# Up projections of a conv-GLU feed-forward layer by seven half-size products, in a float32 kernel on one NeuronCore

## The chip, the cores and the metric

One Trainium2 chip, one of its cores. The kernel computes two model blocks one behind the other in float32, in one launch. The metric is device microseconds of one execution of the program, from repeated runs; a smaller number is better. The chip's engines that occur here: TensorE (PE; its weight loads are listed as PEld), VectorE (DVE), ScalarE (ACT), GpSimd (POOL) and SyncE (SP), whose queue issues the DMAs.

## The reference

The first block (attention, retention and a mixture of experts) is not touched. The second block has two layers on 512 tokens of width 1024; each layer is a mixer, a layer norm, and the feed-forward part that the change is about:

```python
DEPTH_2 = 2; D_MODEL = 1024; SEQ = 512; D_FF = 2816; FFN_CONV = 3

def conv_glu_ffn(x, w_up, w_fconv, b_fconv, w_down):
    a, g = jnp.split(x @ w_up, 2, axis=-1)        # x [1, 512, 1024], w_up [1024, 5632]
    g = causal_dwconv(g, w_fconv, b_fconv)        # three taps along the tokens, per channel
    return (jax.nn.silu(g) * a) @ w_down          # w_down [2816, 1024]

h = layer_norm(ALPHA * h + mix, ln1_g[l], ln1_b[l])
f = conv_glu_ffn(h, w_up[l], w_fconv[l], b_fconv[l], w_down[l])
h = layer_norm(ALPHA * h + f, ln2_g[l], ln2_b[l])
```

`a` are called the values, `g` the gates, and `silu(g) * a` the hidden rows. Everything is float32.

## The kernel before, in words

Five engines run their own instruction lists, held together by semaphores. In `layers_block` each engine goes through the two layers in the same order: mixer, layer norm, feed-forward part (`pe_ffn`, `act_ffn`, `dve_ffn`, then `pool_down` and `dve_down`). `need(name, n)` waits until a semaphore has reached n in this layer, and does so once for each value. `own.do(ins)` waits on VectorE for an instruction of its own; `own(ins)` only counts it.

**Up projections.** The inner dimension of 2816 is cut into NJ = 22 tiles of 128 channels. `m.aT` holds the layer norm's result transposed, as 8 blocks (KT) of 128 input channels by 512 tokens. For tile j, `pe_ffn` (matmul at L2571) runs 8 matmuls for the gates into one bank and 8 for the values into another, each with 128x128 of w_up as the weights and 512 tokens as columns: 16 matmuls. A float32 matmul appears in the trace as two weight loads and two matmul records. Tiles use banks 0 and 1, or 2 and 3, in turn; TensorE waits for `f_gcopy` (gates copied) and `f_hid` (hidden row made) of two tiles before. In tile 0 the last 128 tokens come apart, behind the layer norm's last transposes. At the end of a tile's gates TensorE raises `f_g`, at the end of its values `f_a`.

ScalarE (`act_ffn`) copies the gates to `m.gp` (L2625), and makes SiLU of the convolution's result in `m.gs` (L2629). VectorE (`dve_ffn`) makes the convolution with three instructions (L2641 to L2643), and the hidden row `m.hidT[:, j, :]` with one (L2649), which reads the values from their bank. GpSimd is idle after it has finished the layer norm's rows (L1909, L1910, `pool_ln_rows`).

**Weights.** The SP queue (`sp_ffn`) loads w_up in 11 chunks of two tiles, 2 x 1024 KB each (L2474, L2475), into three slots in turn; chunk c waits for `f_a` of tile 2(c-3)+1. Rows (of 128 channels) 10 to 21 of w_down come as chunks 11 to 13 of 2048 KB through the same slots (L2480), chunk 13 after the last tile; rows 0 to 9 (KE = 10) come behind chunk 4, as 3584 and 1536 KB into `m.wd` (L2482, L2483).

**Down products.** They are already made by seven products of halves: the table SEVEN gives for each product which halves (of tokens, of the inner dimension) of the left operand are added or subtracted, which halves (inner dimension, output) of the right one, and to which quarters of the result the product goes with which sign. Products are accumulated over 11 pairs of rows, in the order `pairs(i)`; a pair is two matmuls of 512 columns, four records. VectorE sums halves of hidden rows (`dve_hid_sums`, L2686; the first four pairs already in tile 10), GpSimd sums halves of weights (`pool_down`, L2667, after the last hidden row, with six buffers `m.bsum` that lie over the convolution's buffers), VectorE adds the products from the banks to `m.h` (`dve_down`, L2704, L2706). Product i uses banks 4 and 5, 6 and 7, 2 and 3, 0 and 1 in turn. The matmul is at L2593.

## Time and profile before

| | us |
|---|---|
| runs: median of 3 (lowest, highest) | 3326.09 (3324.59, 3326.73) |
| profiled execution, its own time | 3328.42 |
| its span | 3326.6 |
| PE busy, share of span | 2857.9, 86% |
| DVE, ACT, POOL busy | 751.8, 462.2, 408.2 |
| mean granted TensorE clock | 0.928 |

The profile has a page (busy time of each engine, 40 slices of the span, DMA queues, the chain of work that ended last, the costliest groups of instructions) and a trace that can be asked by line, by stretch and in order of time. Times count from the span's start. Matmuls are pipelined and the ends of their records are modelled, so the spacing of their starts says more than their durations. A granted clock of 1.00 is 2.4 GHz, 0.50 is 1.2 GHz. The layers' up projections stand at about 2155 to 2461 and 2876 to 3182 us, the down products behind each.

### The profile page before, as it was taken

Reading aid. Unit: us, or ns where it says so; the run is one execution under the profiler, and the core shown is the slowest. Engines: PE = TensorE matmul, PEld = TensorE weight load, DVE = VectorE, ACT = ScalarE, POOL = GpSimd, SP = SyncE. Lnnn points to the kernel's source line nnn. Section 1 sums busy time; section 2 is a strip of 40 time slices with the busy share of each in tenths; the row PEclk is TensorE's granted clock in tenths of the full one; section 3 lists DMA queues with packets and bytes.
Section 4 is the critical chain, followed back from the end, with each engine's and each line's share of the span. In section 5 each row is a group of like instructions: output and inputs, shape, how many; then the busy total and the mean of one; then the engine's idle time right before and its main releaser. Section 6 shows DMA issues by size and latency. Waiting matters only on the chain. (4 is left out here: it accounts for less than half of the span.)

```text
span 3326.6 us, 29164 instructions
## 1 busy us (share of the span) xinstructions
PE 2857.9 (86%) x11870; PEld 1567.5 (47%) x11870; DVE 751.8 (23%) x1885; ACT 462.2 (14%) x1050; POOL 408.2 (12%) x357
## 2 busy tenths in 40 slices
PE   8999999999856565565655899999999999999998
PEld 7888666446722232222322654444444655444443
DVE  2222222101401010010010423322134224212145
ACT  1222232110100000000000223110000222100000
POOL 1101023100100000000000400110026200200044
PEclk9999999999877787777877998999999998999999
DMA  5111221121599999999999511132210311142200
GB/s 210 58 71 71 77 77 51 63 76 57 232 428 428 428 429 428 428 428 428 429 428 427 181 65 64 42 131 79 93 61 0 128 53 50 56 143 92 81 34 25
DMA packets 142087, 592.74 MB, mean 178 GB/s; under 512 B 17186, under 2 KB 88354, under 8 KB 114722
## 3 DMA queue, kind: packets, MB, share of 16 engines
q1 hardware_dynamic: 134674, 574.56, 43.6%
q10 hardware_dynamic: 5120, 8.39, 0.7%
q0 software_dynamic: 2192, 8.39, 0.7%
q8 instruction: 70, 1.15, 0.1%
q14 instruction: 31, 0.25, 0.0%
HBM read 572.37 MB, written 16.84 MB: 177 GB/s over the span
## 5 line engine op out<-in xcount | busy, mean ns | idle before, releaser
L2571 PE MATMUL bank<-arena 128*128 128x512 f32 (+2 forms) x1472 | 608.9, 576 | 9.1 <-DVE arena L1866 9.1
L1240 PE MATMUL bank<-arena 128*32 128x512 f32 x2048 | 294.6, 739 | 347.2 <-DMA arena<-in_moe_w 346.1
L2571 PEld LDWEIGHTS bank<-arena 128*128 128x128 f32 x1472 | 275.8, 191 | 340.3 <-issue 330.4
L429 PE MATMUL bank<-arena 128*128 128x384 f32 x1280 | 431.8, 490 | 1.0 <-PEq L861 1.0
L429 PEld LDWEIGHTS bank<-arena 128*128 128x128 f32 x1280 | 297.9, 238 | 105.9 <-issue 6.0
L1240 PEld LDWEIGHTS bank<-arena 128*32 128x32 f32 x2048 | 81.3, 132 | 559.8 <-issue 559.8
L2593 PE MATMUL bank<-arena 128*128 128x512 f32 x616 | 265.2, 592 | 0.0
L1985 PE MATMUL bank<-arena 128*128 128x512 f32 (+3 forms) x736 | 251.2, 499 | 1.5 <-DVE arena L1866 1.5
L2667 POOL TENSOR_TENSOR arena<-arena 128x512 f32<-128x512 f32 x110 | 148.5, 1355 | 636.0 <-DVE arena L2649 579.1
L1985 PEld LDWEIGHTS bank<-arena 128*128 128x128 f32 x736 | 138.2, 190 | 103.5 <-issue 70.0
L2593 PEld LDWEIGHTS bank<-arena 128*128 128x128 f32 x616 | 116.3, 189 | 147.1 <-issue 145.4
L1499 DVE TENSOR_TENSOR arena<-bank,arena 64x512 f32<-64x512 f32 x32 | 33.4, 1043 | 598.5 <-ACT arena L1329 598.5
L1259 PE MATMUL bank<-arena 128*32 128x512 f32 x1024 | 122.5, 620 | 17.3 <-ACT arena L1333 17.3
L2822 POOL DMA_INDIRECT arena<-y_slots,arena x8 | 8.7, 1082 | 984.4 <-POOLq L1533 982.3
L2641 DVE TENSOR_SCALAR arena<-arena 128x512 f32<-128x512 f32 x44 | 24.7, 561 | 455.8 <-ACT arena L2625 455.8
L1225 PEld LDWEIGHTS bank<-arena 128*128 128x128 f32 x1024 | 116.1, 192 | 12.7 <-issue 12.6
L1225 PE MATMUL bank<-arena 128*128 128x128 f32 x1024 | 119.1, 277 | 0.0
L1329 ACT ACTIVATE arena<-bank 64x512 f32<-64x512 f32 x32 | 18.9, 592 | 719.3 <-PE bank L1240 719.3
L2172 PE MATMUL bank<-arena 128*128 128x512 f32 x256 | 111.6, 592 | 1.4 <-ACT arena L2277 1.4
L425 PE MATMUL bank<-arena 128*128 128x512 f32 x256 | 110.9, 593 | 0.0
L2625 ACT ACTIVATE arena<-bank 128x512 f32<-128x512 f32 x44 | 26.3, 598 | 522.9 <-PE bank L2571 522.9
L629 DVE TENSOR_TENSOR arena<-bank,arena 128x256 f32<-128x256 f32 x64 | 27.2, 426 | 309.9 <-PE bank L429 309.9
(316 smaller groups left out, 2567.5 us busy)
## 6 DMA issues: line engine op xcount, KB each, us to landing
arena<-in_moe_w SPq DMA_DIRECT2D x192, 2048.0 KB, 24.4
arena<-in_w_up SPq DMA_DIRECT2D x44, 1024.0 KB, 7.7
arena<-in_w_in SPq DMA_DIRECT2D x22, 1536.0 KB, 6.8
arena<-in_w_down SPq DMA_DIRECT2D x6, 2048.0 KB, 7.7
arena<-in_w_in SPq DMA_DIRECT2D x8, 1024.0 KB, 5.6
y_slots<-arena ACTq DMA_DIRECT2D x64, 128.0 KB, 8.2
arena<-in_w_in SPq DMA_DIRECT2D x4, 2048.0 KB, 8.8
arena<-in_w_out SPq DMA_DIRECT2D x4, 2048.0 KB, 8.5
```

The costliest lines, as they stand in the source:

```text
L425: ins = pe.matmul(banks[s % 2][:, :], w[:, k, tile(b)], m.aT[:, k, :], start=(k == 0), stop=(k == KT - 1))
L429: ins = pe.matmul(banks[s % 2][:, 0:CW], rows, w[:, k, :], start=(k == 0), stop=(k == KT - 1))
L629: dve.tensor_tensor(m.ra[n % 2], x, cos, ALU.mult)
L1225: ins = pe.matmul(banks[5 + d // 4][:, tile(d % 4)], m.hn[:, t, tile(d)], m.G[:, t, :], start=(t == 0), stop=(t == T - 1))
L1240: ins = pe.matmul(banks[pr][q:q + CAP, :], m.xt[:, k, c:c + CAP], up_view(m, slots[2 * e2 + up])[:, k, :], start=(k == 0), stop=(k == KT - 1))
L1259: ins = pe.matmul(banks[3 + pr][q:q + CAP, :], m.ht[:, f, CAP * e2:CAP * e2 + CAP], down_view(m, slots[4 + e2])[:, f, 512 * half:512 * hal ...
L1499: dve.tensor_tensor(by_place(m.hid[0:64, :], FF // P), spread(banks[pr][64:128, :], FF // P), spread(m.hs[64:128, :], FF // P), ALU.mult)\
L1985: ins = pe.matmul(out, a, b, start=(i == 0), stop=(i == len(terms) - 1))
L2172: ins = pe.matmul(row_banks(banks, 2 * l + 1, t)[half][:, :], m.mixT[:, k, tile(t)], slot_view(m, i)[:, k, :], start=(first and k == ks[0] ...
L2571: ins = pe.matmul(banks[2 * (j % 2) + half][:, part], w[:, k, c0:c0 + P], m.aT[:, k, part], start=(k == 0), stop=(k == KT - 1))
L2593: ins = pe.matmul(banks[seven_banks(i) + u][:, :], rows[:, tile(u)], weights, start=(n == 0), stop=(n == NPAIR - 1))
L2667: pool.tensor_tensor(m.bsum[g % len(m.bsum)], down_weights(m, l, p, *a), down_weights(m, l, p, *b), SIGN[op])\
```

## The change

Tiles 2 to 21 of each layer (NPLAIN = 2 stay as they were) use the table SEVEN as well. The three cut dimensions are the tokens (two halves of 256), the input channels (two halves of four blocks), and the output, whose halves are the values and the gates of one tile. A product is four accumulating matmuls of 256 columns, 28 in a tile. They run in the order UP = 1, 3, 0, 5, 2, 6, 4 into four banks, two products in a bank; even tiles take banks 4 to 7 and odd ones 0 to 3.

- VectorE makes five sums of token halves once per layer (`m.tsum`, 1024 elements each), before its first convolution.
- GpSimd makes five sums of weights per tile (`pool_up`, 512 elements each from four runs of 128, eight buffers `m.wsum`), 100 per layer.
- ScalarE copies two products of a tile, each to both token halves: one to the gates (`m.gp`), one to the values (`m.hidT[:, j, :]`).
- VectorE adds the other products from the banks to these, six instructions per tile; the hidden row then has both operands in SBUF, and it is made one tile later in VectorE's list, before these additions. The sums for the first four down pairs move from tile 10 to tile 15.
- `m.tsum` lies where rows of w_down were. Rows 0 to 4 are loaded behind chunk 4 (1024 and 1536 KB), rows 5 to 9 (2560 KB) behind chunk 13, after the last tile. The down products take pairs 2, 3 and 4 last (PAIRS); the seventh product's order stays.
- Behind the last tile, TensorE waits for the hidden row 20 before the first down product, and as before for the last one at product 2.

The diff, with unchanged parts cut:

```diff
@@ -1574,6 +1574,7 @@
     m = persistent(arena)
     sp = Space(arena, m.free)
     at = sp.at
+    m.z_at = at
     m.z = sp(T, D)
     n = Space(arena, at)
     m.qnT, m.knT = n(MH, S), n(MH, S)
@@ -1644,10 +1645,13 @@
     m.gs = [f(S) for _ in range(2)]
+    m.wsum = [Space(arena, m.z_at + S * i)(KT // 2, P) for i in range(8)]
     m.bsum = [Space(arena, m.ff_gp + S * i)(S) for i in range(6)]
     m.asum = [f(2 * P) for _ in range(4)] + [m.aT[:, k, 2 * P:] for k in range(KT)]
     raw = Space(arena, m.raw_at)
-    m.wd = [raw(7, D), f(3, D)]
+    m.tsum = [Space(arena, m.raw_at + D * i)(KT // 2, 2 * P) for i in range(5)]
+    m.wd = [raw(5, D), raw(2, D), f(3, D)]
     assert raw.at <= m.slots_at
     return m
@@ -1663,8 +1667,8 @@
...
-    "f_in0": 16 * 9, "f_in1": 16 * 9, "f_in2": 16 * 7, "f_e": 32, "f_zero": 1, "f_g": 22, "f_a": 22, "f_gcopy": 22,
-    "f_conv": 22, "f_silu": 22, "f_hid": 22, "f_down": 14, "f_down_k": 70, "f_as": 55, "f_bs": 55, "f_evac": 24,
+    "f_in0": 16 * 9, "f_in1": 16 * 9, "f_in2": 16 * 7, "f_e": 48, "f_zero": 1, "f_g": 62, "f_a": 22, "f_gcopy": 42,
+    "f_conv": 22, "f_silu": 22, "f_hid": 22, "f_down": 14, "f_down_k": 70, "f_as": 55, "f_ts": 5, "f_bs": 155, "f_evac": 24,
 }
...
@@ -2478,9 +2482,12 @@
             k = KE + 4 * (c - 11)
             v = m.slots[s].rearrange("p (k n) -> p k n", n=D)
             sp.dma_start(v, down[:, k:k + 4, :]).then_inc(G[f"f_in{c % 3}"], 16)
+            if c == 13:
+                need("f_a", NJ)
+                sp.dma_start(m.wd[0], down[:, 5:KE, :]).then_inc(G["f_e"], 16)
         if c == 4:
-            sp.dma_start(m.wd[0], down[:, 0:7, :]).then_inc(G["f_e"], 16)
-            sp.dma_start(m.wd[1], down[:, 7:KE, :]).then_inc(G["f_e"], 16)
+            sp.dma_start(m.wd[1], down[:, 0:2, :]).then_inc(G["f_e"], 16)
+            sp.dma_start(m.wd[2], down[:, 2:5, :]).then_inc(G["f_e"], 16)
         if c == 8:
             ln_rows(sp, m, G, A, 2 * l + 2)
@@ -2512,8 +2519,45 @@
 NBOTH = 6
+PAIRS = (0, 1, 5, 6, 7, 8, 9, 10, 2, 3, 4)
 def pairs(i):
-    return LAST_PAIRS if i == 6 else tuple(range(NPAIR))
+    return LAST_PAIRS if i == 6 else PAIRS
+NPLAIN = 2
+UP = (1, 3, 0, 5, 2, 6, 4)
+UP_SUMMED = [i for i in UP if len(SEVEN[i][1]) > 1]
+def up_banks(j):
+    return 0 if j % 2 else 4
+def up_done(j, b):
+    if b == 3:
+        return "f_a", j + 1
+    return "f_g", (NPLAIN + 3 * (j - NPLAIN) + b + 1 if j >= NPLAIN else j + 1)
+def copied(j, part):
+    return NPLAIN + 2 * (j - NPLAIN) + part + 1 if j >= NPLAIN else j + 1
+def up_weights(m, l, j, parity, half):
+    c0 = 256 * half + P * (j % 2)
+    return slot_view(m, ffn_slot(l, j // 2))[:, 4 * parity:4 * parity + 4, c0:c0 + P]
+def up_rows(m, half, parity):
+    return m.aT[:, 4 * parity:4 * parity + 4, 2 * P * half:2 * P * half + 2 * P]
 def done(i, n):
@@ -2537,17 +2581,19 @@
 def down_weights(m, l, p, parity, half):
     k = 2 * p + parity
     cols = slice(512 * half, 512 * half + 512)
-    if k < 7:
-        return m.wd[0][:, k, cols]
+    if k < 2:
+        return m.wd[1][:, k, cols]
+    if k < 5:
+        return m.wd[2][:, k - 2, cols]
     if k < KE:
-        return m.wd[1][:, k - 7, cols]
+        return m.wd[0][:, k - 5, cols]
     v = m.slots[ffn_slot(l, 11 + (k - KE) // 4)].rearrange("p (k n) -> p k n", n=D)
     return v[:, (k - KE) % 4, cols]
 def need_weights(need, p):
     if p < KE // 2:
-        need("f_e", 32)
+        need("f_e", 32 if p < 2 else 48)
     else:
         c = 11 + (2 * p - KE) // 4
         need(f"f_in{c % 3}", ffn_in(c))
@@ -2556,7 +2602,7 @@
 def pe_ffn(pe, need, ln, m, G, banks, l):
     for t in range(3):
         pe_ln_ready(ln, 2 * l + 1, t)
-    for j in range(NJ):
+    for j in range(NPLAIN):
         c = j // 2
         need(f"f_in{c % 3}", ffn_in(c))
         w = slot_view(m, ffn_slot(l, c))
@@ -2573,6 +2619,33 @@
                 if part.stop == S:
                     ins.then_inc(G[name], 1)
+    def up_product(j, n):
+        i = UP[n]
+        x, w, _ = SEVEN[i]
+        if len(x) > 1:
+            need("f_ts", SUMMED_A.index(i) + 1)
+            rows = m.tsum[SUMMED_A.index(i)]
+        else:
+            rows = up_rows(m, *x[0])
+        if len(w) > 1:
+            g = len(UP_SUMMED) * (j - NPLAIN) + UP_SUMMED.index(i)
+            need("f_bs", g + 1)
+            weights = m.wsum[g % len(m.wsum)]
+        else:
+            weights = up_weights(m, l, j, *w[0])
+        out = banks[up_banks(j) + n // 2][:, 256 * (n % 2):256 * (n % 2) + 256]
+        for k in range(KT // 2):
+            ins = pe.matmul(out, weights[:, k, :], rows[:, k, :], start=(k == 0), stop=(k == KT // 2 - 1))
+        if n % 2 or n == 6:
+            ins.then_inc(G[up_done(j, n // 2)[0]], 1)
+    for j in range(NPLAIN, NJ):
+        need(f"f_in{(j // 2) % 3}", ffn_in(j // 2))
+        if j > NPLAIN:
+            need("f_hid", j - 1)
+        for n in range(len(UP)):
+            up_product(j, n)
     def product(i, n, u):
         p = pairs(i)[n]
         x, w, _ = SEVEN[i]
@@ -2585,7 +2658,7 @@
             rows = hid_rows(m, p, *x[0])
         if len(w) > 1:
             g = NPAIR * SUMMED_B.index(i) + n
-            need("f_bs", g + 1)
+            need("f_bs", len(UP_SUMMED) * (NJ - NPLAIN) + g + 1)
             weights = m.bsum[g % len(m.bsum)]
         else:
             need_weights(need, p)
@@ -2597,9 +2670,9 @@
         elif u:
             ins.then_inc(G["f_down_k"], 1)
+    need("f_hid", NJ - 1)
     for i in range(len(SEVEN)):
         if i == 2:
-            need("f_gcopy", NJ)
             need("f_hid", NJ)
         if i >= 4:
             need("f_evac", added(i - 4, 1))
@@ -2620,34 +2693,85 @@
 def act_ffn(act, need, m, G, banks):
     for j in range(NJ + 1):
         if j < NJ:
-            need("f_g", j + 1)
+            need(*up_done(j, 0))
             need("f_conv", j - 1)
-            act.activation(m.gp[j % 2][:, 2:], banks[2 * (j % 2) + 1][:, :], ACT.Copy).then_inc(G["f_gcopy"], 1)
+            if j < NPLAIN:
+                act.activation(m.gp[j % 2][:, 2:], banks[2 * (j % 2) + 1][:, :], ACT.Copy).then_inc(G["f_gcopy"], 1)
+            else:
+                for part, dst in enumerate((m.gp[j % 2][:, 2:], m.hidT[:, j, :])):
+                    src = banks[up_banks(j)][:, 256 * part:256 * part + 256]
+                    act.activation(dst.rearrange("p (a b) -> p a b", a=2), src.unsqueeze(1).broadcast_to([P, 2, 256]),
+                                   ACT.Copy).then_inc(G["f_gcopy"], 1)
         if j:
             need("f_conv", j)
             need("f_hid", j - 2)
             act.activation(m.gs[(j - 1) % 2], m.gconv[(j - 1) % 2], ACT.Silu).then_inc(G["f_silu"], 1)
-def dve_ffn(dve, need, own, m, G, banks):
+def dve_ffn(dve, need, own, ln, m, G, banks, l):
+    for name in ("n_a0", "n_a1"):
+        ln(name, T * (2 * l + 2))
+    for i, x in enumerate(SUMMED_A):
+        p, op, q = SEVEN[x][0]
+        dve.tensor_tensor(m.tsum[i], up_rows(m, *p), up_rows(m, *q), SIGN[op]).then_inc(G["f_ts"], 1)
     need("f_zero", 1)
-    for j in range(NJ + 1):
-        if j == 10:
-            dve_hid_sums(dve, need, m, G, 0, range(4))
-        if j < NJ:
-            gc, gp = m.gconv[j % 2], m.gp[j % 2]
-            need("f_gcopy", j + 1)
-            need("f_silu", j - 1)
-            own.do(dve.tensor_scalar(gc, gp[:, 0:S], m.wf[:, j, 0:1], m.wf[:, j, 3:4], ALU.mult, ALU.add))
-            own.do(dve.scalar_tensor_tensor(gc, gp[:, 1:1 + S], m.wf[:, j, 1:2], gc, ALU.mult, ALU.add))
-            dve.scalar_tensor_tensor(gc, gp[:, 2:2 + S], m.wf[:, j, 2:3], gc, ALU.mult, ALU.add)\
-               .then_inc(G["f_conv"], 1)
-        if j:
-            i = j - 1
-            need("f_a", i + 1)
-            need("f_silu", i + 1)
-            dve.tensor_tensor(m.hidT[:, i, :], banks[2 * (i % 2)][:, :], m.gs[i % 2], ALU.mult)\
-               .then_inc(G["f_hid"], 1)
+    def hidden(j):
+        need("f_silu", j + 1)
+        if j < NPLAIN:
+            need("f_a", j + 1)
+            a = banks[2 * (j % 2)][:, :]
+        else:
+            a = m.hidT[:, j, :]
+        dve.tensor_tensor(m.hidT[:, j, :], a, m.gs[j % 2], ALU.mult).then_inc(G["f_hid"], 1)
+    for j in range(NJ):
+        gc, gp = m.gconv[j % 2], m.gp[j % 2]
+        need("f_gcopy", copied(j, 0))
+        if j >= NPLAIN:
+            if j == 15:
+                dve_hid_sums(dve, need, m, G, 0, range(4))
+            hidden(j - 1)
+            b1, b2, b3 = (banks[up_banks(j) + b] for b in (1, 2, 3))
+            lo, hi = slice(0, 256), slice(256, S)
+            g, a = gp[:, 2:], m.hidT[:, j, :]
+            need("f_gcopy", copied(j, 1))
+            need(*up_done(j, 1))
+            own(dve.tensor_tensor(g, g, b1[:, :], ALU.add))
+            n = own(dve.tensor_tensor(a[:, lo], a[:, lo], b1[:, lo], ALU.subtract))
+            need(*up_done(j, 2))
+            own.wait(n)
+            own(dve.tensor_tensor(g[:, hi], g[:, hi], b2[:, hi], ALU.subtract))
+            n = own(dve.tensor_tensor(a, a, b2[:, :], ALU.add))
+            need(*up_done(j, 3))
+            own.wait(n)
+            own(dve.tensor_tensor(g[:, hi], g[:, hi], b3[:, lo], ALU.add))
+            own.do(dve.tensor_tensor(a[:, lo], a[:, lo], b3[:, lo], ALU.add))
+        need("f_silu", j - 1)
+        own.do(dve.tensor_scalar(gc, gp[:, 0:S], m.wf[:, j, 0:1], m.wf[:, j, 3:4], ALU.mult, ALU.add))
+        own.do(dve.scalar_tensor_tensor(gc, gp[:, 1:1 + S], m.wf[:, j, 1:2], gc, ALU.mult, ALU.add))
+        dve.scalar_tensor_tensor(gc, gp[:, 2:2 + S], m.wf[:, j, 2:3], gc, ALU.mult, ALU.add).then_inc(G["f_conv"], 1)
+        if 0 < j < NPLAIN:
+            hidden(j - 1)
+    hidden(NJ - 1)
+def pool_up(pool, need, ln, m, G, l):
+    v = 2 * l + 1
+    ln("n_turn", 2 * T * (v + 1))
+    ln("n_h", T * (v + 1))
+    g = 0
+    for j in range(NPLAIN, NJ):
+        need(f"f_in{(j // 2) % 3}", ffn_in(j // 2))
+        for i in UP_SUMMED:
+            a, op, b = SEVEN[i][1]
+            if g >= len(m.wsum):
+                o = g - len(m.wsum)
+                need(*up_done(NPLAIN + o // len(UP_SUMMED), UP.index(UP_SUMMED[o % len(UP_SUMMED)]) // 2))
+            pool.tensor_tensor(m.wsum[g % len(m.wsum)], up_weights(m, l, j, *a), up_weights(m, l, j, *b), SIGN[op])\
+                .then_inc(G["f_bs"], 1)
+            g += 1
 def pool_down(pool, need, ln, m, G, l):
...
```

## Rows read from the trace of the kernel before

**Rows 1.** Page, part 1 (busy us, share, instructions) and part 4 (chain).

```profile
PE 2857.9 (86%) x11870; PEld 1567.5 (47%) x11870; DVE 751.8 (23%) x1885; ACT 462.2 (14%) x1050; POOL 408.2 (12%) x357
...
PE bank L2571 18%; PE bank L2593 8%; PE bank L1985 7%; PE bank L2172 3%; PE bank L2138 1%; PE bank L2139 1%; PE bank L842 1%; PE bank L2112 1%; PE bank L2123 1%; PE bank L2145 0%; PE bank L1838 0%; PE bank L2156 0%; PE bank L2132 0%; PE bank L2098 0%; DVE arena L1866 0%
```

**Rows 2.** Busy time by stretch (its ends and length, then the columns named first).

```profile
core 0: us, PE busy (x) PEld busy (x) DVE busy (x) ACT busy (x) POOL busy (x), PEclk, DMA share, GB/s
792.00:848.00 56.00, 55.68 (x256) 48.29 (x256) 6.51 (x16) 0.00 (x0) 0.00 (x0) 1.00 0.13 43
2171.00:2461.00 290.00, 290.00 (x693) 129.76 (x693) 59.62 (x91) 26.09 (x45) 2.10 (x1) 1.00 0.28 94
```

**Rows 3.** PE in order of time: start, us, line, shape, count; both layers.

```profile
2169.63 292.21 PE L2571 MATMUL bank<-arena 128*128 128x128 f32 x704 [1.55 <-DVE arena L1866]
2461.68 113.55 PE L2593 MATMUL bank<-arena 128*128 128x512 f32 x264
...
2890.51 292.21 PE L2571 MATMUL bank<-arena 128*128 128x128 f32 x704 [1.55 <-DVE arena L1866]
```

**Rows 4.** SP queue in order of time: the loads behind tiles 1 and 3.

```profile
2187.21 0.37 SPq L2474 DMA_DIRECT2D arena<-in_w_up  x1
...
2214.67 0.37 SPq L2474 DMA_DIRECT2D arena<-in_w_up  x1
...
2215.71 1.96 SPq L2482 DMA_DIRECT2D arena<-in_w_down  x1
2217.71 2.60 SPq L2483 DMA_DIRECT2D arena<-in_w_down  x1
```

**Rows 5.** Line L1039: durations min/median/max in ns, first and last start.

```profile
L1039 PE MATMUL bank<-arena x256: 377/378/454, 792.1 to 847.4; 128*128 128x256 f32 x128
```

**Rows 6.** Groups of instructions, shapes apart: additions that read a bank.

```profile
L629 DVE TENSOR_TENSOR arena<-bank,arena 128x256 f32<-128x256 f32 x64 | 27.2, 426 | 309.9 <-PE bank L429 309.9
```

**Rows 7.** Order of time in a middle up tile, ACT and DVE.

```profile
2441.77 0.62 ACT L2629 ACTIVATE arena<-arena 128x512 f32<-128x512 f32 x1
2441.91 0.55 DVE L2641 TENSOR_SCALAR arena<-arena 128x512 f32<-128x512 f32 x1 [11.01 <-ACT arena L2625]
...
2442.49 0.75 DVE L2642 SCALAR_TENSOR_TENSOR arena<-arena 128x512 f32<-128x512 f32 x1
```

**Rows 8.** Order of time behind the last up tile, DVE and POOL.

```profile
2461.88 0.69 DVE L2649 TENSOR_TENSOR arena<-bank,arena 128x512 f32<-128x512 f32 x1 [3.50 <-PE bank L2571]
...
2462.49 8.86 DVE L2686 TENSOR_TENSOR arena<-arena 128x256 f32<-128x256 f32 x7
...
2462.65 8.41 POOL L2667 TENSOR_TENSOR arena<-arena 128x512 f32<-128x512 f32 x6 [289.55 <-DVE arena L2649]
```

**Rows 9.** Order of time at two places where DVE and POOL run together.

```profile
2170.75 2.36 POOL L1910 TENSOR_TENSOR arena<-arena 128x1024 f32<-128x1024 f32 x1
...
2172.39 0.99 DVE L2641 TENSOR_SCALAR arena<-arena 128x512 f32<-128x512 f32 x1 [2.91 <-ACT arena L2625]
...
2537.51 1.28 POOL L2667 TENSOR_TENSOR arena<-arena 128x512 f32<-128x512 f32 x1 [0.45 <-PE bank L2593]
...
2537.81 0.68 DVE L2704 TENSOR_TENSOR arena<-arena,bank 128x512 f32<-128x512 f32 x1
```

**Rows 10.** Line L779, a POOL addition, operand in four runs; columns as group 5.

```profile
L779 POOL TENSOR_TENSOR arena<-arena x8: 1273/1277/1304, 449.0 to 645.8; 128x512 f32<-128x512 f32 x8
```

**Rows 11.** DMA issues, 2150 to 2600: count, KB, median us to landing.

```profile
arena<-in_w_down SPq DMA_DIRECT2D x3, 2048.0 KB, 7.8
arena<-in_w_down SPq DMA_DIRECT2D x1, 3584.0 KB, 16.8
...
arena<-in_w_down SPq DMA_DIRECT2D x1, 1536.0 KB, 18.6
```

**Rows 12.** PE's first up records in time, and their stretch (as group 2).

```profile
2154.95 12.25 PE L2571 MATMUL bank<-arena 128*128 128x384 f32 x32 [3.01 <-DVE arena L1866]
...
2155.00:2158.00 3.00, 3.00 (x7) 1.75 (x8) 1.46 (x1) 1.24 (x1) 2.92 (x2) 0.70 1.09 354
```

More of the change, by code:

```diff
@@ L2842, in pool_layers @@
         pool_ln_rows(pool, own, m, G, ln, 2 * l + 1)
+        pool_up(pool, need, ln, m, G, l)
         pool_down(pool, need, ln, m, G, l)
@@ L2897, in dve_layers @@
         dve_ln_turned(dve, m, G, banks, ln, 2 * l + 1, 3)
-        dve_ffn(dve, need, own, m, G, banks)
+        dve_ffn(dve, need, own, ln, m, G, banks, l)
         dve_down(dve, need, own, ln, m, G, banks, l)
```

## The prediction

> **What bounds the kernel now.** I read the page first. TensorE is busy 86% of the span, and in the chain that ended last the line of the up projections, L2571, has the largest share of one line, 18%, with the down products (L2593, 8%) behind it [rows 1]. Next the stretches: from 2171 to 2461 us, nearly all of the up projections of layer 0, TensorE shows 290.00 of 290.00 us busy, a granted clock of 1.00 (2.4 GHz), VectorE 59.62, ScalarE 26.09, GpSimd 2.10, and DMA at 0.28 [rows 2]. The order of time says the same: 704 matmul records of L2571 stand back to back for 292.21 us, in both layers alike [rows 3]. So these stretches are TensorE's alone; whatever shortens its instruction stream shortens the kernel, as long as the other engines still fit beside it. The stretch has much spare room on them, and that is what the change spends.
>
> The measure of a tile is in the SP queue: the loads that wait for tiles 1 and 3 start at 2187.21 and 2214.67 us, so two tiles take 27.46 and one 13.73 us [rows 4]. A float32 matmul leaves two records; a tile of 16 matmuls has 32, so 429 ns for one of 512 columns.
>
> **TensorE's part.** Twenty of 22 tiles per layer go from 32 records of 512 columns to 7 x 4 x 2 = 56 records of 256 columns. The trace has such records: those of L1039 (128x256, a new weight load before each, waits before each group of 16) start from 792.1 to 847.4 us, so 55.3 / 255 = 216.9 ns each, at clock 1.00 [rows 2, 5]. A tile then takes 56 x 216.9 = 12.15 us, 1.58 less, and 40 tiles 63.3 us. Lower bound of the spacing: half a 512-column record, 214.6 ns, 12.02 us a tile, 68.6 us in all. Upper bound: L1039's first record took 454 ns where the others took 378 [rows 5]; if each of the seven products, each with its own waits, began with those 76 ns, a tile would take 12.68 us and the gain be 42 us. I take 216.9, for L1039 crossed 16 groups with it.
>
> The margin to watch is the weight load. It takes 48.29 / 256 = 189 ns [rows 2]; beside a record of 429 ns it leaves much room, beside 217 ns only 28. L1039 shows that it still hides. *The Trainium skill, "TensorE: Matmul & The Clock Gate", "The mechanism", says that weight loads overlap with running matmuls only when the row groups differ (all loads here use 128 rows); its "Step-by-step: what each phase is for" also lets a load go ahead into a background buffer. The rows of L1039 go against the first and with the second; what the first would make of the time stands with the rivals.*
>
> **VectorE's part.** Per tile it gains six additions that read a bank: two of 512 and four of 256 elements. Such additions took 0.68 us for 512 elements (L2704) and 0.426 for 256 (L629) [rows 6, 9], so 1.36 + 1.70 = 3.1 us. It keeps the convolution, 0.55 + 0.75 + 0.75, and the product with the gates, 0.69 [rows 7, 8]: 2.74, and 5.8 in all, under half of 12.15. The product now reads two SBUF operands instead of a bank and one. That matters beside GpSimd's five sums per tile. Where both run, seven SBUF additions of VectorE took 8.86 us, one per GpSimd instruction (six in 8.41) [rows 8], though one alone takes 0.43; a TENSOR_SCALAR of 0.55 took 0.99 and ended 0.27 after GpSimd's had; but an addition that read a bank took 0.68 inside a GpSimd instruction [rows 9]. So the six new additions go free of this, and the four SBUF instructions may each wait for one GpSimd instruction. *The Trainium skill, "SBUF — State Buffer", section "SBUF: two separate sides", has this as an exclusive lock on a port pair, held for a whole instruction, between GpSimd and a VectorE instruction with two SBUF inputs or in a two-port mode. By that rule alone the two engines' SBUF work would stand in a row, some 6.4 + 2.7 us a tile, and the three us of bank additions beside it: still under 12.15.*
>
> **GpSimd's part.** A sum of 512 elements took 1.28 us at L779, where one input is four runs of 128 with gaps [rows 10], as both are here; five make 6.4 us a tile, at most 1.4 each beside VectorE [rows 8], 7.0. It runs ahead: with eight buffers, the sum for the first product of a tile may start seven us into the tile two before. Its first sums wait for the layer norm's rows, whose last instruction ends at 2170.75 + 2.36 = 2173.1 us [rows 9]; tile 2 starts at 2187.2, and VectorE's five sums of tokens (1024 elements, by 0.43 for 256 at most 1.7 us each and a GpSimd instruction between) end near 2185. They are first needed two products into tile 2, at 2190.7. Nothing here reaches TensorE.
>
> **The loop of waits.** TensorE starts a tile once the hidden row of the tile two before is done. Take tile A, whose last up matmul ends at 0, and tile B behind it, from 0 to 12.15. VectorE does A's last two bank additions until 1.0 and the convolution until 3.2 (4.5 if the GpSimd sum that is released at 0 holds it once). ScalarE has in its order first the two copies of B's first products, which are there at 2 x 8 x 0.217 = 3.5, and does them until 4.7, then A's SiLU until 5.3 (0.62 us for 512 elements [rows 7], taken for the copies too). Two GpSimd sums start at 3.5 and hold A's product with the gates until 6.2; it ends at 6.9. The tile after B asks for it at 12.15. That is 5.2 us of slack, and one GpSimd instruction is 1.3: TensorE stays the bound. In tile 15 the first four sums for the down products come in between, by 8.86 / 7 = 1.27 each 5.1 us at most: still done at 12.0. What queues behind VectorE's waits for the banks is its own later work of the same tile; nobody else waits for that.
>
> **The change-over to the down products.** Called t, when the last up matmul ends. Before, VectorE needed only one 0.69 us instruction behind it [rows 8]. Now two additions of 0.43, the convolution 2.1, SiLU 0.62 and the product 0.69 follow, with the hand-overs (0.2 us before the row of 0.69, TensorE's records ending at 2461.68, [rows 3, 8]): done at about t + 4.7. The fifth pair of the first down product needs it (four pairs are summed earlier), and a pair of four records takes 1.72 us, so at t + 6.9; its sum is done at t + 5.2, the next four follow by 1.42 and are needed by 1.72. Hidden, with 1.7 us to spare; GpSimd's down sums start at t + 4.7 and are needed at t + 18.9. The weights are closer. Rows 18 to 21 are loaded at t as before, but the order of the pairs wants them at t + 6 x 1.72 = 10.3; the 2048 KB land in 7.8 us [rows 11]. Behind them in the same queue, 2560 KB that had been loaded during the up tiles: 1536 KB landed (2217.71 + 18.6) - (2215.71 + 16.8) = 3.8 us after the 3584 KB before it [rows 4, 11], so 2560 take 6.3, and land at t + 14.2. The ninth pair wants them at t + 13.7. I charge 0.5 us a layer, 1.0 in all.
>
> **Sum.** The profiled execution has a span of 3326.6 and took 3328.4 us; after: 3326.6 - 63.3 + 1.0 = 3264.3 and 3266.1. It stands 2.3 us over the median of the runs, 3326.1, from which the same sum gives 3263.8. I forecast **3264 us**, ratio 1.019.
>
> **The rivals.**
> - *The loads collide at the change-over.* If the two transfers share the queue instead of following each other, the first also lands near t + 14, 3.8 us too late for the seventh pair. A gap of 3.01 us at the start of the up tiles was followed by a stretch of 3 us at a granted clock of 0.70, between the levels of 1.2 and 2.4 GHz [rows 12], 0.9 us lost; it may go on as long again, so 1.8. That is 5.6 a layer instead of 0.5: 3274. For: both are issued at the same moment. Against: the 1536 KB landed after the 3584, not with it.
> - *VectorE sets the pace.* 5.8 us of work and each of five GpSimd sums holding it once for 1.3 makes 12.3; with the time between ten dependent instructions (0.03 each [rows 7]) 12.6, and 0.45 x 40 = 18 us go: 3282. Half that, when only some sums hold it: 3273. Against: the order above leaves VectorE idle for several us in each tile.
> - *Each product starts late*, 76 ns each: 3285, as above. Against: L1039's other 15 groups.
> - *Slower: the weight load no longer hides.* Place: the load before each 256-column record. It decides from 13.73 / 56 = 245 ns a record. In full, load and matmul one after the other, 189 + 217 = 406 ns make 22.7 us a tile, 9.0 x 40 = 360 us more: 3686. Half exposed, 0.31 a record, it is 3.6 x 40 = 145 more. Against: 256 records of L1039 in a row. For: DMA was light then (43 GB/s, [rows 2]) and here it is not. I give the full case 0.01, by the evidence of L1039, and the half 0.02. *The full case is what the row-group sentence of "TensorE: Matmul & The Clock Gate" in the Trainium skill would do here.*
> That the seven products are fewer instructions of a kind that the trace has, is certain from the diff; the change cannot fail to do that.
>
> **Chances.** Forecast 0.70 (own range 3257 to 3267, from the bound of 214.6 ns and one us of stall a layer more); colliding loads 0.12; VectorE's pace 0.08; late starts 0.06; exposed loads 0.03 (0.01 and 0.02); 0.01 for a stall that happens to eat all. The range 3257 to 3279 leaves out the late starts, the exposed loads and half of VectorE's case. Two tenths of a per cent, 6.7 us, is what a measurement of this kernel can tell from no change. Faster 0.96, same 0.01, slower 0.03.
>
> **What would show it.** Up tiles 12.15 us apart in the SP queue's loads (24.3 per pair); PE records of the new product line with 217 ns of spacing, weight loads busy 87% of the stretch; no row of waits of PE on VectorE's additions or GpSimd's sums; VectorE's hidden product and convolution longer than alone, up to 1.3 us more; at the change-over a gap under 1 us, released by a DMA. The prediction is wrong if the spacing is over 220 ns, if PE waits in every tile, or if that gap is over 3 us.

## The result, and the profile after

| | before | after |
|---|---|---|
| median of the runs beside each other, us | 3325.3 | 3260.9 (3258.5 to 3265.4) |
| ratio after to before | | 0.9821, 95% interval 0.9807 to 0.9834 |
| profiled execution: span, own time, us | 3326.6, 3328.4 | 3263.4, 3265.4 |

The two medians are 64 us apart, and their quotient is 0.9806; the ratio in the table, which has the interval, says 1.8%, 60 us. A second series of five runs of the same changed kernel, in the last set of experiments, gave a median of 3260.3 beside 3320.9, 61 us less, and a ratio of 0.9814 (0.9801 to 0.9828). So the gain is 60 to 64 us. Forecast were 3264 us, 62 below the 3326.1 from which the prediction started.

TensorE after, in order of time from the last plain tiles to the first down products of layer 0; it answers to [rows 3]:

```profile
2169.12 17.54 PE L2617 MATMUL bank<-arena 128*128 128x128 f32 x64 [1.55 <-DVE arena L1870]
2186.51 242.43 PE L2638 MATMUL bank<-arena 128*128 128x256 f32 x1120
2428.78 13.90 PE L2666 MATMUL bank<-arena 128*128 128x512 f32 x32
2443.43 99.89 PE L2666 MATMUL bank<-arena 128*128 128x512 f32 x232 [0.76 <-DMA arena<-in_w_down]
```

L2638 is the new product line. Its 1120 records stand from 2186.51 to 2428.78 without a gap: 242.27 / 20 = 12.11 us a tile, 216.3 ns a record. Then eight pairs, and one gap of 0.76 us that ends with a load. The SP queue gives the same spacing, to be set beside [rows 4]:

```profile
2186.70 0.37 SPq L2478 DMA_DIRECT2D arena<-in_w_up  x1
...
2210.93 0.37 SPq L2478 DMA_DIRECT2D arena<-in_w_up  x1
```

Two tiles take 24.23 us instead of 27.46. Busy time in a middle stretch, columns as in [rows 2]:

```profile
2190.00:2425.00 235.00, 235.00 (x1088) 205.68 (x1087) 128.32 (x198) 32.10 (x60) 116.96 (x92) 1.00 0.31 103
```

TensorE 235.00 of 235.00 us, its weight loads 205.68, VectorE 128.32 (6.6 us a tile), ScalarE 32.10, GpSimd 116.96, clock 1.00. GpSimd's are 92 sums of 1.28 us, so 6.4 us in a tile that has all five; it runs ahead and is done with the last of the layer's 100 sums at 2410.7. VectorE's groups in the same stretch, each with count, busy time, mean of one and the idle time before it:

```profile
L2726 DVE TENSOR_TENSOR arena<-arena 128x512 f32<-128x512 f32 x19 | 26.2, 1380 | 35.8 <-ACT arena L2708 35.8
L2751 DVE TENSOR_SCALAR arena<-arena 128x512 f32<-128x512 f32 x19 | 15.3, 804 | 0.7
L2752 DVE SCALAR_TENSOR_TENSOR arena<-arena 128x512 f32<-128x512 f32 x19 | 14.3, 753 | 0.7
L2753 DVE SCALAR_TENSOR_TENSOR arena<-arena 128x512 f32<-128x512 f32 x19 | 14.3, 753 | 0.7
L2740 DVE TENSOR_TENSOR arena<-arena,bank 128x512 f32<-128x512 f32 x20 | 13.8, 688 | 9.6 <-PE bank L2638 9.6
L2744 DVE TENSOR_TENSOR arena<-arena,bank 128x256 f32<-128x256 f32 x19 | 8.0, 422 | 43.4 <-PE bank L2638 43.4
```

The hidden product (L2726) has doubled to 1.38 us and the first convolution instruction (L2751) takes 0.80 instead of 0.55, both beside GpSimd's sums; the other two convolution instructions and the bank additions have their old durations. The time by which such an instruction is longer than alone is called a hold below: here 0.69 and 0.26, 0.9 us a tile. VectorE stands idle 2.3 us a tile for the banks of L2744 alone (43.4 / 19). Nothing on TensorE waits for it.

### The profile page after: what moved, and what is told of

The parts are those of the page before. It is cut to its first block and busy times, and to the rows that moved or that the text cites. A ratio compares the mean times of both kernels' runs of the same rounds, so it can differ in the third digit from the quotient of the medians.

```text
span 3263.4 us, 31740 instructions
## 1 busy us (share of the span) xinstructions
PE 2792.0 (86%) x12830; PEld 1749.1 (54%) x12830; DVE 938.0 (29%) x2135; ACT 481.7 (15%) x1090; POOL 674.0 (21%) x557
## 3 DMA queue, kind: packets, MB, share of 16 engines
q8 instruction: 78, 1.28, 0.2%
## 5 line engine op out<-in xcount | busy, mean ns | idle before, releaser
L2638 PE MATMUL bank<-arena 128*128 128x256 f32 x2240 | 484.9, 378 | 0.0
L2638 PEld LDWEIGHTS bank<-arena 128*128 128x128 f32 x2240 | 424.1, 189 | 61.3 <-issue 1.0
L429 PEld LDWEIGHTS bank<-arena 128*128 128x128 f32 x1280 | 298.0, 238 | 105.9 <-issue 6.0
L2772 POOL TENSOR_TENSOR arena<-arena 128x512 f32<-128x512 f32 x200 | 263.9, 1330 | 210.7 <-PE bank L2638 210.4
L2666 PEld LDWEIGHTS bank<-arena 128*128 128x128 f32 x616 | 116.2, 189 | 148.4 <-issue 147.1
L1989 PEld LDWEIGHTS bank<-arena 128*128 128x128 f32 x736 | 138.9, 191 | 105.4 <-issue 74.2
L2791 POOL TENSOR_TENSOR arena<-arena 128x512 f32<-128x512 f32 x110 | 148.6, 1356 | 96.9 <-PE bank L2666 51.6
L1259 PE MATMUL bank<-arena 128*32 128x512 f32 x1024 | 123.9, 626 | 17.4 <-ACT arena L1333 17.4
L757 POOL TENSOR_TENSOR arena<-arena 128x256 f32<-128x256 f32 x64 | 46.8, 731 | 378.3 <-DVE arena L631 378.3
L1225 PEld LDWEIGHTS bank<-arena 128*128 128x128 f32 x1024 | 116.5, 193 | 12.7 <-issue 12.6
```

What stands on the lines that cost most here:

```text
L429: ins = pe.matmul(banks[s % 2][:, 0:CW], rows, w[:, k, :], start=(k == 0), stop=(k == KT - 1))
L1225: ins = pe.matmul(banks[5 + d // 4][:, tile(d % 4)], m.hn[:, t, tile(d)], m.G[:, t, :], start=(t == 0), stop=(t == T - 1))
L1259: ins = pe.matmul(banks[3 + pr][q:q + CAP, :], m.ht[:, f, CAP * e2:CAP * e2 + CAP], down_view(m, slots[4 + e2])[:, f, 512 * half:512 * hal ...
L1989: ins = pe.matmul(out, a, b, start=(i == 0), stop=(i == len(terms) - 1))
L2638: ins = pe.matmul(out, weights[:, k, :], rows[:, k, :], start=(k == 0), stop=(k == KT // 2 - 1))
L2666: ins = pe.matmul(banks[seven_banks(i) + u][:, :], rows[:, tile(u)], weights, start=(n == 0), stop=(n == NPAIR - 1))
```

## The experiments

Each kernel is the changed one with one edit unless it says otherwise; ratios are to the kernel before, run beside it.

**1. Eight narrow products in the old kernel.** What is gained by seven, and what does the narrow form cost?

```diff
-                for k in range(KT):
-                    c0 = 256 * half + P * (j % 2)
-                    ins = pe.matmul(banks[2 * (j % 2) + half][:, part], w[:, k, c0:c0 + P], m.aT[:, k, part],
-                                    start=(k == 0), stop=(k == KT - 1))
+                for cols in (part,) if j < 2 else (slice(0, 256), slice(256, S)):
+                    for k in range(KT):
+                        c0 = 256 * half + P * (j % 2)
+                        ins = pe.matmul(banks[2 * (j % 2) + half][:, cols], w[:, k, c0:c0 + P], m.aT[:, k, cols],
+                                        start=(k == 0), stop=(k == KT - 1))
```

> The kernel before, with the up matmuls of tiles 2 to 21 cut into halves of 256 columns: all eight products, no sums, the full computation. Theory (the gain is one product in eight, and the narrow records cost next to nothing): 64 records of 216.3 ns make 13.84 us a tile instead of 13.73, so 40 x 0.11 = 4 us slower than before, about 3330. Rival (the weight load shows beside narrow records once it is looked at alone, or the gain came from the narrow form and the other banks): over 220 ns a record, 14.1 us and more, over 15 us slower; or faster than before.

Median 3327.9 beside 3323.7; ratio 1.0011 (1.0000 to 1.0022). TensorE in order of time:

```profile
2163.41 293.81 PE L2572 MATMUL bank<-arena 128*128 128x128 f32 x1344 [1.55 <-DVE arena L1866]
2457.06 13.47 PE L2594 MATMUL bank<-arena 128*128 128x512 f32 x31
```

The first 64 of these 1344 records (rest of tile 0, tile 1) take 17.4 us, as in the changed kernel's 2169.12 to 2186.51. So 1280 records take 293.65 - 17.4 = 276.3 us: 215.8 ns each, 13.81 us a tile, 0.08 over 13.73, 3 us in all. The narrow records cost nearly nothing; the whole gain comes from leaving out the eighth product.

**2. No weight sums.** TensorE takes `up_weights(m, l, j, *w[0])` where it took a sum, so that five products of a tile have wrong weights, and `pool_up` goes (with it the 100 up sums in the counts of `f_bs`):

```diff
-            need("f_bs", g + 1)
-            weights = m.wsum[g % len(m.wsum)]
+            weights = up_weights(m, l, j, *w[0])
...
-        pool_up(pool, need, ln, m, G, l)
```

> The changed kernel without GpSimd's sums for the up products: TensorE takes the first half of the weights in their place, so those five products of each tile have wrong weights; all else is done. Theory (TensorE sets the pace, the sums and what they do to VectorE are hidden): 3261 within 3 us, tiles 12.11 us apart, but VectorE's convolution back at 0.55, 0.75 and 0.75 us and the hidden product at 0.69. Rival (GpSimd's sums cost TensorE or VectorE time that shows): several us faster.

Median 3262.7, ratio 0.9810 (0.9793 to 0.9826), the changed kernel's. VectorE in the middle of the up tiles:

```profile
L2750 DVE SCALAR_TENSOR_TENSOR arena<-arena 128x512 f32<-128x512 f32 x19 | 14.3, 753 | 0.7
L2724 DVE TENSOR_TENSOR arena<-arena 128x512 f32<-128x512 f32 x19 | 13.2, 695 | 40.4 <-ACT arena L2706 40.4
L2749 DVE TENSOR_SCALAR arena<-arena 128x512 f32<-128x512 f32 x19 | 10.4, 548 | 0.7
```

The hidden product is back at 0.695 and the TENSOR_SCALAR at 0.548. So the holds of 0.69 and 0.26 us a tile come from GpSimd's sums, 0.94 together, and all of it is hidden.

**3. Every sum twice.** The first of the two is waited for before the second starts.

```diff
+            own.do(pool.tensor_tensor(m.wsum[g % len(m.wsum)], up_weights(m, l, j, *a), up_weights(m, l, j, *b), SIGN[op]))
             pool.tensor_tensor(m.wsum[g % len(m.wsum)], up_weights(m, l, j, *a), up_weights(m, l, j, *b), SIGN[op])\
```

> The changed kernel with every GpSimd sum of the up products made twice, ten per tile. Both theories see GpSimd as the bound. Exclusive access (one engine stands still while the other works in SBUF): 10 x 1.28 and what VectorE's four SBUF instructions hold, about 1.4, and the hand-overs, 14.7 us a tile, 40 x 2.6 = 104 us slower than the changed kernel, about 3365. Rival (they only slow each other a little): 10 x 1.33 = 13.3 us a tile, 48 us, about 3309.

Median 3333.8 (3332.7 to 3344.8), ratio 1.0028 (1.0017 to 1.0039). The profiled execution is the longest of them, 3344.8. In it, TensorE:

```profile
2218.80 7.23 PE L2638 MATMUL bank<-arena 128*128 128x256 f32 x32 [0.82 <-POOL arena L2773]
2226.83 5.46 PE L2638 MATMUL bank<-arena 128*128 128x256 f32 x24 [0.80 <-POOL arena L2773]
2233.10 7.24 PE L2638 MATMUL bank<-arena 128*128 128x256 f32 x32 [0.82 <-POOL arena L2773]
```

14.30 us a tile (2218.80 to 2233.10), each tile waiting twice for GpSimd (POOL). GpSimd and VectorE where they meet:

```profile
2311.05 1.53 POOL L2773 TENSOR_TENSOR arena<-arena 128x512 f32<-128x512 f32 x1
2312.54 1.72 POOL L2772 TENSOR_TENSOR arena<-arena 128x512 f32<-128x512 f32 x1
2314.34 1.61 POOL L2773 TENSOR_TENSOR arena<-arena 128x512 f32<-128x512 f32 x1
2315.91 1.27 POOL L2772 TENSOR_TENSOR arena<-arena 128x512 f32<-128x512 f32 x1
...
2311.48 1.64 DVE L2752 SCALAR_TENSOR_TENSOR arena<-arena 128x512 f32<-128x512 f32 x1
2313.16 1.65 DVE L2753 SCALAR_TENSOR_TENSOR arena<-arena 128x512 f32<-128x512 f32 x1
```

A sum alone takes 1.27 us; those that meet one of VectorE's SBUF instructions take 0.26 to 0.45 more, 1.4 us in the ten sums of a tile, and VectorE's take 1.65 where they take 0.75 alone. 12.7 + 1.4 and the hand-overs between the doubled sums give the 14.3. The ends of these instructions fit exclusive access, for they take turns though the spans overlap: GpSimd at 2312.58, VectorE at 2313.12, GpSimd at 2314.26, VectorE at 2314.81, GpSimd at 2315.95. The forecast total is another matter: the median is 73 us over the changed kernel's, between the 104 of this theory and the 48 of its rival, and it is the tile of the trace (14.3, not 13.3) that decides. 3365 was too high by 20 even against the profiled run, because a tile takes 0.4 us less than the 14.7 expected, and because the eight buffers carry TensorE through the first two to three tiles of a layer at full pace. Why most runs are some 11 us shorter than the profiled one isn't settled: no trace of such a run exists. With ten sums GpSimd is the bound; with five it has nearly half of its time over.

**4. Down pairs in their old order.**

```diff
-PAIRS = (0, 1, 5, 6, 7, 8, 9, 10, 2, 3, 4)
+PAIRS = tuple(range(11))
```

> The changed kernel with the down pairs in the order 0 to 10 again. Theory: the third pair wants at t + 3.4 us what lands at t + 14.5 behind the last up matmul, so a gap of 11 us per layer in place of 0.8, and about 1.7 us more of it at a low clock: 2 x 12 = 24 us slower than the changed kernel, about 3285. Rival (the gap also delays what VectorE and GpSimd do later, or the clock stays down longer): over 30 us. Rival (the sums behind it catch up and give some back): under 15 us.

Median 3287.5, ratio 0.9880 (0.9864 to 0.9897). TensorE in order of time at the change-over:

```profile
2428.95 3.60 PE L2666 MATMUL bank<-arena 128*128 128x512 f32 x8
2443.74 26.64 PE L2666 MATMUL bank<-arena 128*128 128x512 f32 x55 [11.19 <-DMA arena<-in_w_down]
```

And its busy time by stretch behind the gap, columns as in [rows 2]:

```profile
2444.00:2447.00 3.00, 3.00 (x4) 1.21 (x4) 0.00 (x0) 0.00 (x0) 3.00 (x3) 0.50 0.00 0
2447.00:2450.00 3.00, 3.00 (x5) 1.19 (x4) 0.00 (x0) 0.00 (x0) 1.60 (x2) 0.61 0.00 0
2450.00:2453.00 3.00, 3.00 (x8) 1.32 (x7) 0.00 (x0) 0.00 (x0) 0.00 (x0) 1.00 0.02 5
```

The gap is 11.19 us, 10.4 more than in the changed kernel, and behind it the granted clock is 0.50, then 0.61, then 1.00: the lower level of 1.2 GHz until it rises again, which costs 1.5 + 1.2 = 2.7 us. In layer 1 the gap is 10.69 us, 9.9 more, and the clock 0.78 over the 13.6 us behind it, 3.0 us lost. Together 13.1 and 12.9 us; the two profiled spans differ by 26.4, the medians by 26.5 (by 24.8 from experiment 2, which was run beside this one and has the changed kernel's time). The new order of the pairs is a necessary part of the change, worth about 26 of its 60 to 64 us. Nothing behind the gap gave time back.

**5. The late load in two pieces.**

```diff
-                sp.dma_start(m.wd[0], down[:, 5:KE, :]).then_inc(G["f_e"], 16)
+                sp.dma_start(m.wd[0][:, 0:1, :], down[:, 5:6, :]).then_inc(G["f_w"], 16)
+                sp.dma_start(m.wd[0][:, 1:5, :], down[:, 6:KE, :]).then_inc(G["f_e"], 16)
```

(pair 2 then waits for `f_w`, pairs 3 and 4 for `f_e`)

> The changed kernel with the 2560 KB load at the change-over in two: first 512 KB, the one row that the ninth pair lacks, then 2048 KB. Theory: the small piece lands near t + 9.5 us, before its pair wants it at t + 13.8, the rest near t + 14.6, before t + 15.5: the gap of 0.76 us in each layer goes, 1.5 us in all, which a trace shows and the median hardly. Rival (a second issue costs more than the order saves, or the late rows still come too late): a gap of the same size one pair later.

Once more, with the changed kernel beside it:

> The changed kernel with the load at the change-over in two pieces once more, to compare with the changed kernel on the same chip. Theory: 1.5 us faster than it, 0.05%, inside the spread of the runs; the gap behind the load is gone again. Rival: over 3 us faster, so that the pieces gain something beyond the gap.

> The changed kernel once more, beside the next one on the same chip. Every theory: ratio to before 0.981, as measured.

First time: median 3258.0, ratio 0.9802 (0.9780 to 0.9823); again, beside the changed kernel: 3258.5 to its 3260.3, ratios 0.9805 (0.9791 to 0.9818) and 0.9814 (0.9801 to 0.9828). TensorE in order of time:

```profile
2184.28 242.43 PE L2642 MATMUL bank<-arena 128*128 128x256 f32 x1120
2426.55 43.96 PE L2670 MATMUL bank<-arena 128*128 128x512 f32 x102
```

No gap is left at the change-over, in either layer of either series. The changed kernel's second profiled execution has it, and longer in layer 0:

```profile
2442.09 99.89 PE L2666 MATMUL bank<-arena 128*128 128x512 f32 x232 [1.75 <-DMA arena<-in_w_down]
```

In layer 1 it is 0.39 there, where the first execution had 0.82. So the length of the gap varies, 0.39 to 1.75 us, 1.6 and 2.1 us for both layers together. The intervals overlap, so the medians' 1.8 us are not shown to be a gain; what the traces show is that the gaps are gone. It has the lowest median of the kernels here that compute the whole result, by less than the spread.

**6. The convolution three times.** More work for VectorE, the same result:

```diff
+        for _ in range(2 if j >= NPLAIN else 0):
+            own.do(dve.tensor_scalar(gc, gp[:, 0:S], m.wf[:, j, 0:1], m.wf[:, j, 3:4], ALU.mult, ALU.add))
+            own.do(dve.scalar_tensor_tensor(gc, gp[:, 1:1 + S], m.wf[:, j, 1:2], gc, ALU.mult, ALU.add))
+            own.do(dve.scalar_tensor_tensor(gc, gp[:, 2:2 + S], m.wf[:, j, 2:3], gc, ALU.mult, ALU.add))
```

> The changed kernel with the convolution of tiles 2 to 21 made three times over, 2 x 2.05 us more work on VectorE per tile, the same result. VectorE is busy 6.6 us a tile in the changed kernel. Theory (it has 5.5 us to spare, and what GpSimd holds it adds about one more): 11.8 us against 12.11, hidden, 3261 to 3266. Rival (each further SBUF instruction is held by a GpSimd sum too, so VectorE has nearly no slack): 13 us a tile and more, over 3296.

Median 3351.8, ratio 1.0090 (1.0072 to 1.0108): slower than the kernel before. The theory of the spare time fell. TensorE and VectorE in order of time:

```profile
2305.88 12.38 PE L2638 MATMUL bank<-arena 128*128 128x256 f32 x56 [2.35 <-DVE arena L2726]
...
2309.35 0.75 DVE L2753 SCALAR_TENSOR_TENSOR arena<-arena 128x512 f32<-128x512 f32 x1
2310.14 1.65 DVE L2754 SCALAR_TENSOR_TENSOR arena<-arena 128x512 f32<-128x512 f32 x1
2311.83 1.38 DVE L2752 TENSOR_SCALAR arena<-arena 128x512 f32<-128x512 f32 x1
2313.24 1.72 DVE L2753 SCALAR_TENSOR_TENSOR arena<-arena 128x512 f32<-128x512 f32 x1
2315.00 0.75 DVE L2754 SCALAR_TENSOR_TENSOR arena<-arena 128x512 f32<-128x512 f32 x1
...
2317.16 1.65 DVE L2757 SCALAR_TENSOR_TENSOR arena<-arena 128x512 f32<-128x512 f32 x1
```

A tile takes 14.7 us (the hidden products start at 2304.91 and 2319.58), and TensorE stands idle once before most of its tiles, 28.7 us from 2200 to 2450; the profile gives half of that (14.6) to the hidden product and names nothing for the rest. In such a tile four convolution instructions are longer than alone, by 0.90, 0.83, 0.97 and 0.90, and the hidden product (0.91 us) by 0.22: 3.8 us of holds where the changed kernel has 0.94. VectorE's own list makes 9.9 us, 0.4 between instructions, 0.8 until SiLU is there; with the 3.8, 14.9. The next two runs take the two causes apart.

**7. The convolution three times, without weight sums,** and **twice, with them.** (The edits of 6 and 2 together; the edit of 6 with `range(1 ...)`.)

> The convolution three times over, but without GpSimd's sums for the up products (TensorE takes the first half of the weights, so those products are wrong). Theory (the 3.8 us of holds made VectorE the bound, not its own work): 3.1 + 3 x 2.05 + 0.69 + 0.4 + 0.8 = 11.1 us a tile, under 12.11, so hidden: 3261 to 3264, about 90 us less than with the sums. Rival (VectorE's own order and its wait for SiLU make the 14.7 us): over 3320, as with the sums.

> The changed kernel with the convolution of tiles 2 to 21 made twice, 2.05 us more work on VectorE per tile, the same result. With it three times, VectorE had no idle time left and four of GpSimd's five sums per tile held one of its SBUF instructions by 0.83 to 0.97 us, 3.8 us in all. Theory of the holds: VectorE's list alone is 3.1 + 2 x 2.05 + 0.69, 0.3 between them and 0.8 until SiLU is there, 9.0 us; with 3.8 of holds 12.8 us a tile, with three held 11.9. So at the edge: between 3261 and 3290, and more of VectorE's instructions held than the changed kernel shows (0.8 us a tile). Theory of the spare time alone (6.6 + 2.05 = 8.7 us, much under 12.11): 3261, and holds as before.

Three times without sums: median 3265.8, ratio 0.9834 (0.9819 to 0.9849), 86 us less than with the sums. Its up tiles take 12.12 us. Its median is 5 us over the changed kernel's; its trace shows two gaps of 2.2 us at the change-over, where VectorE's work behind the last tile is 4.1 us longer, in place of the load's 1.6 to 2.1 us in all. That explains about half of the 5, and the rest is inside the spread of the runs. Twice with sums: median 3259.0, ratio 0.9815 (0.9800 to 0.9830), the changed kernel's time. Busy time by stretch, 6 first, then 7 without sums, then 7 with them (VectorE is the third number with a count, POOL the fifth):

```profile
2200.00:2450.00 250.00, 221.34 (x966) 187.23 (x966) 228.11 (x278) 29.73 (x52) 125.74 (x84) 0.97 0.27 91
```

```profile
2200.00:2400.00 200.00, 200.00 (x926) 175.30 (x925) 158.75 (x270) 27.50 (x48) 0.00 (x0) 1.00 0.31 104
```

```profile
2200.00:2400.00 200.00, 200.00 (x926) 175.21 (x925) 164.06 (x221) 28.58 (x50) 114.38 (x83) 1.00 0.32 109
```

And VectorE's groups in 7 with the sums, where `L2756` is the second instruction of the last convolution:

```profile
L2756 DVE SCALAR_TENSOR_TENSOR arena<-arena 128x512 f32<-128x512 f32 x17 | 28.0, 1648 | 0.6
L2726 DVE TENSOR_TENSOR arena<-arena 128x512 f32<-128x512 f32 x16 | 14.8, 923 | 11.5 <-ACT arena L2708 11.5
```

By 12.11 us a tile, VectorE is busy 9.6 us when nothing holds it and that hides completely; with one extra convolution and the sums it is busy 9.9, holds among them, and that hides too. So it was the holds that made VectorE the bound. Their sum isn't fixed: 0.9 us a tile with one convolution, 2.3 with two (2 x 0.90 on the second and third instruction of the last convolution, 0.25 on the first of the added one, 0.23 on the hidden product), 3.8 with three. The expectation for two, which took over the 3.8 and made 11.9 to 12.8 us a tile of it, was too high. As VectorE's idle time goes, more of GpSimd's five sums meet one of its SBUF instructions: two are held with one convolution, four with two, five with three.

**8. Six products.** Product 6 is left out of the result:

```diff
         for n in range(len(UP)):
-            up_product(j, n)
+            if n != 5:
+                up_product(j, n)
```

(and the count of bank 2 is raised at n == 4)

> The changed kernel without the product whose weights are a plain quarter (number 6), six per tile: its contribution is missing from the result, and VectorE adds what stands in the bank. Theory (TensorE alone paces the tile, the other engines have over 1.7 us of slack): 48 x 216.3 ns = 10.38 us a tile, 69 us faster than the changed kernel, 3192. Rival (another engine is close behind): less than 60 us.

Median 3193.2, ratio 0.9603 (0.9582 to 0.9625); 207.67 us for 20 tiles, 10.38 each, to the nanosecond per record what was expected. The other engines keep up with a tile 1.73 us shorter.

**9. Ten tiles per layer by seven products.**

```diff
-NPLAIN = 2
+NPLAIN = 12
```

> The changed kernel with 12 plain tiles per layer in place of 2, so 10 by seven products. Theory (the gain is the same in every tile, and what stands around them, the sums of tokens and the late load, costs under 2 us): 20 x 1.62 = 32 us less than before, about half of the changed kernel's gain, ratio to before 0.990. Rival (part of the gain or of a hidden cost comes once per layer): off from the half by over 6 us.

Median 3292.8, ratio 0.9907 (0.9889 to 0.9925). That is half of the changed kernel's gain (0.9814 would give 0.9907). In the trace the ten more plain tiles of layer 0 take 13.73 us each and the ten by seven products 12.11. So the gain comes per tile; the interval leaves room for up to 6 us that would come once per layer.

## Why the prediction was right

- **TensorE is the bound, and its stream gets shorter.** Right: no gap in 1120 records, six products as fast as counted (8), half the tiles half the gain, within the interval (9).
- **Spacing.** 216.9 ns taken from L1039, 216.3 measured; 12.11 for 12.15 us a tile, so 1.62 x 40 = 65 us for 63.3. The late starts of 76 ns per product don't exist.
- **The weight load hides.** Loads of 189 ns beside records of 216.3: 205.68 / 235 = 88% busy (87% said), with GpSimd, VectorE and DMA at work; experiment 1 shows the same with 215.8 ns. *The row-group sentence in "The mechanism" of the Trainium skill's page "TensorE: Matmul & The Clock Gate" would have made a tile 22.7 us, by the prediction's estimate; these 2240 records of 128-row loads go against it, as L1039 did.*
- **VectorE's part.** Bank additions 0.68 and 0.42 us, untouched by GpSimd: right. Where one was followed, the hidden product ran from 2409.91 for 1.40 us, behind a tile that had ended at 2186.51 + 18 x 12.11 = 2404.5: 6.8 us after its end; 6.9 had been said. But the words "under half of 12.15" and "5.2 us of slack" say too much of the margin: the 4.1 us that experiment 6 adds were not hidden. The rival had it better: with every sum holding VectorE once it put the tile at 12.6. Experiment 6 shows that case in another kernel, with 0.8 to 1.0 us per hold, not 1.3. At that price the changed kernel's own list, with a hold for each of the five sums, would be 5.8 + 0.3 + 0.8 + 5 x 0.9 = 11.4 us, an estimate: under 12.11, by 0.7. So the margin was there even in the rival's case, but it was small. In the run only 0.9 us of holds came about, because VectorE still has idle time for the sums to fall into, and experiment 7 (twice) shows that for 2.05 us more.
- **GpSimd's part.** Sums 1.28 us each as said; five of VectorE's token sums took 12.15 us, ended at 2181.2 and not near 2185, long before 2190.7.
- **The change-over.** Right in kind, one load behind the other and a gap that ends with the second. The second was issued at 2429.38, 0.6 us behind the last up matmul (t), and landed 13.9 us behind its issue, so at t + 14.5; t + 14.2 had been said, with an issue at t. The gap was 0.76 and 0.82 us in the two layers, 0.5 said: the term was sized about 0.3 a layer too small, and too exact, since the second profiled execution had 1.75 and 0.39. The two loads did not collide. VectorE was done early enough: the last hidden product ran from 2432.59 to 2433.28, t + 4.5 (4.7 said).
- **The sum.** 3263.4 for the span, 3264.3 said: the tiles gave 64.8 us where 63.3 were said and the gaps took 1.6 where 1.0 was said, and 64.8 - 1.6 = 63.2 is the difference of the two profiled spans. The median of 3260.9 is 3 us lower than the forecast, inside the spread of the runs (3258.5 to 3265.4); the profiled run was the slowest of its four. The forecast ratio of 1.019 is before to after; measured it is 1 / 0.9821 = 1.018. That the median came out so close is in part luck: the medians of the kernel before lie between 3319.6 and 3326.1 from series to series.

## What to carry to other kernels

Seven products of halves paid here, where TensorE was the only busy engine: one record in eight goes. The narrower records (256 columns, 216 ns) were still longer than a weight load (189 ns); what shorter ones would do, no run here shows. Put what the sums cost on engines with idle time, and judge that idle time with every possible hold counted: VectorE at 55% was safe, while 4.1 us more work on it, beside GpSimd's sums, made the tile 14.7 us. A buffer that the change takes moves a load, and its order of use must move with it: here about 26 us hung on the order of the pairs.

## What the runs showed of the hardware

- VectorE's SBUF instructions against GpSimd's sums: one such instruction of 0.75 us becomes 1.65 to 1.80, a TENSOR_SCALAR of 0.55 (one operand in SBUF) 0.80 to 1.50, and GpSimd's sum of 1.27 becomes 1.5 to 1.7; instructions that read a bank keep 0.68 and 0.42. *The Trainium skill, "SBUF — State Buffer", "SBUF: two separate sides", calls it an exclusive lock that whichever instruction starts first has for its whole length. That one waits for the other agrees (0.75 to 1.65 us); what the runs add is that the sum of these waits grows from 0.9 to 3.8 us a tile with the work on VectorE, at the same number of GpSimd sums.*
- Behind a gap of 11.19 us TensorE's clock was granted at 0.50 for three us and 0.61 for the next three; it had fallen while the engine stood idle, to 0.62 from 2435 to 2438 (the gap began at 2432.5) and 0.50 behind that. Behind the gaps of 0.76 us and 1.75 us it was 1.00 at once, so the changed kernel's own gap costs its length and no more:

```profile
2443.00:2446.00 3.00, 2.57 (x6) 1.24 (x7) 0.00 (x0) 0.00 (x0) 0.00 (x0) 1.00 0.02 5
```
